# The last two outputs of three projections: whole products in the first half of the contraction, and another bank for the rest of the second token half

## The reference

```
for i in range(2):
    m = mixer_i(rmsnorm(x, norm_mix_pre[i]))           # ends in a projection to 1024
    x = x + rmsnorm(m, norm_mix_post[i])
    f = conv_ffn(rmsnorm(x, norm_ffn_pre[i]))          # ends in a projection to 1024
    x = x + rmsnorm(f, norm_ffn_post[i])
```

## Time and profile before

| | us |
|---|---|
| median of 3 runs | 1428.8 |
| range of the runs | 1427.78 to 1429.37 |
| profiled execution | 1427.95 |
| its span, first to last instruction | 1426.2 |
| PE busy | 1407.8 (99%) |
| DVE busy | 1003.5 (70%) |
| ACT busy | 623.4 (44%) |
| POOL busy | 112.3 (8%) |

### The profile page before, as it was taken

One profiled execution on the slowest core, in us unless ns is written; L12 is line 12 of the kernel. 1 busy time (PEld: TensorE's weight loads), 2 busy tenths in 40 slices (PEclk: granted clock), 3 DMA queues, 4 the chain that ended last, 5 costly groups with the idle time before them and its releaser, 6 DMA issues.

```text
span 1426.2 us, 21715 instructions
## 1 busy us (share of the span) xinstructions
PE 1407.8 (99%) x7526; PEld 1177.3 (83%) x7526; DVE 1003.5 (70%) x1510; ACT 623.4 (44%) x1019; POOL 112.3 (8%) x85
## 2 busy tenths in 40 slices
PE   8999999999999999999999999999999999999997
PEld 6888888888789888888888977777798888888887
DVE  6988888889437888888522676767488888886123
ACT  6666556557334323232323456556653232333221
POOL 0000000000110000000011032232110000000111
PEclk9999999999999999999999999999999999999999
DMA  4433433342231322323233012121212223233231
GB/s 165 180 135 128 147 117 118 136 142 76 83 139 33 102 98 94 103 88 114 102 100 141 31 60 75 59 74 59 93 56 89 97 94 103 89 108 103 102 101 60
DMA packets 37445, 142.34 MB, mean 100 GB/s; under 512 B 4176, under 2 KB 6352, under 8 KB 35344
## 3 DMA queue, kind: packets, MB, share of 16 engines
q1 hardware_dynamic: 37392, 141.63, 28.7%
HBM read 139.38 MB, written 2.23 MB: 99 GB/s over the span
## 4 chain that ended last, share of the span: by engine, by line
PE 94%; DVE 3%; ACT 1%; DMA 1%; issue 1%; SPq 0%; POOL 0%; POOLq 0%; ACTq 0%
PE bank L469 21%; PE bank L471 20%; PE bank L470 20%; PE b_x L469 7%; PE b_x L470 7%; PE b_x L471 7%; PE b_y L1073 1%; PE b_norm L1642 1%; PE b_y L469 1%; PE b_y L471 1%; DVE hn_lo L814 1%; PE b_y L470 1%; PE b_x L1085 1%; PE b_y L1076 1%; DVE mbuf L819 1%; PE b_cb L1602 1%
## 5 line engine op out<-in xcount | busy, mean ns | idle before, releaser
L417 ACT ACTIVATE w_hi<-raw 128x1024 fp32r<-128x1024 f32 (+1 forms) x201 | 222.8, 1108 | 403.2 <-PE bank L471 287.8
L432 DVE TENSOR_TENSOR w_lo<-raw,w_hi 128x1024 fp32r<-128x1024 f32 (+1 forms) x181 | 234.1, 1294 | 229.5 <-ACT w_hi L417 229.4
L469 PE MATMUL bank<-hn_hi,w_hi 128*128 128x512 f32 x848 | 337.2, 398 | 2.2 <-DVE w_lo L432 1.1
L471 PE MATMUL bank<-hn_hi,w_lo 128*128 128x512 f32 x848 | 330.8, 390 | 0.0
L470 PE MATMUL bank<-hn_lo,w_hi 128*128 128x512 f32 x848 | 330.3, 390 | 0.0
L469 PEld LDWEIGHTS bank<-hn_hi,w_hi 128*128 128x128 f32 x848 | 159.2, 188 | 40.0 <-issue 4.5
L471 PEld LDWEIGHTS bank<-hn_hi,w_lo 128*128 128x128 f32 x848 | 159.2, 188 | 33.9
L470 PEld LDWEIGHTS bank<-hn_lo,w_hi 128*128 128x128 f32 x848 | 159.4, 188 | 31.4
L469 PE MATMUL bank<-h_hi,w_hi 128*128 128x512 f32 (+1 forms) x352 | 127.9, 363 | 0.0
L471 PE MATMUL bank<-h_hi,w_lo 128*128 128x512 f32 (+1 forms) x352 | 127.6, 363 | 0.0
L470 PE MATMUL bank<-h_lo,w_hi 128*128 128x512 f32 (+1 forms) x352 | 127.6, 363 | 0.0
(11 more groups left out here) (318 smaller groups left out, 2423.1 us busy)
## 6 DMA issues: line engine op xcount, KB each, us to landing
raw<-w_up SPq DMA_DIRECT2D x80, 512.0 KB, 3.2
raw<-w_mix SPq DMA_DIRECT2D x48, 512.0 KB, 3.3
raw<-w_dn SPq DMA_DIRECT2D x32, 704.0 KB, 4.1
raw<-w_qkv SPq DMA_DIRECT2D x20, 512.0 KB, 3.3
acs_bc<-scratch SPq DMA_DIRECT2D x8, 1024.0 KB, 5.6
ecs_bc<-scratch SPq DMA_DIRECT2D x8, 1024.0 KB, 4.7
raw<-w_sout SPq DMA_DIRECT2D x16, 512.0 KB, 3.2
first_raw<-w_up SPq DMA_DIRECT2D x8, 512.0 KB, 6.3
```

The lines of the kernel that those rows point to most:

```text
L417: nc.scalar.activation(halves_of(ph, j if own else rep, own or first and j < 4)[0], raw_of(ph, rep, first and j < 4), ACT.Copy).then_inc(h ...
L432: nc.vector.tensor_tensor(lo, raw_of(ph, rep, first), hi.bitcast(F32), ALU.subtract).then_inc(lo_made, 1)
L469: nc.tensor.matmul(acc[:], wh, hi, start=first, stop=False)
L471: return nc.tensor.matmul(acc[:], wl, hi, start=False, stop=last)
```

## The change

Three projections (SOUT, DN0, DN1) are concerned. AOUT keeps its accumulators; in its boundary only the order in `wide_start` changes.

- `pair_pe`: the first half of the contraction of outputs 6 and 7 is made by products over all 512 tokens into the output's bank. The rest of token half 0 is added there. The rest of token half 1 begins anew in `b_x`.
- So token half 1 is the sum of two accumulators. ScalarE copies the bank's part to mbuf behind the root of token half 0 (semaphore `kept`). VectorE adds the part in `b_x` to it (`join`), and that is now what counts as the evacuation of the output. ScalarE's square of token half 1 waits for this and reads mbuf.
- `join` 0 stands on VectorE behind the first two new_x of token half 0, `join` 1 behind new_x of chunk 3. At the end of the kernel they stand ahead of the third group of scalings and ahead of the second reciprocal.
- `wide_start`: as `b_x` is read until the joins are done, chunks 0 and 1 are run for units 0 and 1 first, then the statistic of token half 1, then a wait for the evacuations, then chunks 0 and 1 for units 2 and 3.

```diff
         def part_acc(ph, t, s):
-            return acc_of(ph, s)[:, tokens(1)] if t else b_x[:, s, tokens(0)]
+            own = t if ph is AOUT else not t
+            return acc_of(ph, s)[:, tokens(t)] if own else b_x[:, s, tokens(t)]
@@ pair_pe
                     for c in range(tiles):
-                        for t in range(2):
-                            last = product(part_acc(ph, t, s), slot_of(ph, u), c, hi[:, c, tokens(t)],
-                                           lo[:, c, tokens(t)], c == 0, False)
+                        last = product(acc_of(ph, s), slot_of(ph, u), c, hi[:, c, :], lo[:, c, :], c == 0, False)
...
-                                       k == 0, c == tiles - 1)
+                                       c == 0 and (t == 1 or ph is AOUT), c == tiles - 1)
@@ wide_start
-            for c in range(KC):
+            for c in range(2):
+                for j in range(2):
+                    chunk(0, j, c)
+            part_stat(pe, b, 1)
+            pe.wait_ge(evac["out"], nxt.before["out"])
+            for c in range(2):
+                for j in (2, 3):
+                    chunk(0, j, c)
+            for c in range(2, KC):
                 for j in range(4):
                     chunk(0, j, c)
-                if c == 0:
-                    part_stat(pe, b, 1)
@@ boundary_act, take
+                if t and ph is not AOUT:
+                    act.wait_ge(evac["out"], ph.before["out"] + KC - 1 + s)
+                    nc.scalar.activation(sq[:, s, tokens(t)], mbuf[:, 2 * END + s, tokens(t)],
+                                         ACT.Square).then_inc(part_squared, 1)
+                    return
@@ boundary_act, behind part_root(0)
+            if ph is not AOUT:
+                for s in range(2):
+                    nc.scalar.activation(mbuf[:, 2 * END + s, tokens(1)], acc_of(ph, s)[:, tokens(1)],
+                                         ACT.Copy).then_inc(kept, 1)
@@ new, VectorE
+        def join(dve, b, s):
+
+            ph = PH[2 * b - 1]
+            if ph is AOUT:
+                return
+            dve.wait_ge(unit_done, ph.U0 + ph.units - 1 + s)
+            dve.wait_ge(kept, 2 * KEEPS.index(b) + s + 1)
+            nc.vector.tensor_tensor(mbuf[:, 2 * END + s, tokens(1)], mbuf[:, 2 * END + s, tokens(1)],
+                                    b_x[:, s, tokens(1)], ALU.add).then_inc(evac["out"], 1)
@@ boundary_dve
                 new_x(t, 0)
                 new_x(t, 1)
+                if t == 0:
+                    join(dve, b, 0)
                 for m in range(KC):
...
                     if m + 2 < KC:
                         new_x(t, m + 2)
+                    if t == 0 and m == 1:
+                        join(dve, b, 1)
@@ end_dve
                 if t:
+                    join(dve, b, 1)
                     part_diag(dve, b, t)
...
+                    if t == 0 and n == 2:
+                        join(dve, b, 0)
                     for m in steps:
                         scale(m)
```

More of the change, by code:

```diff
@@ L260, in trunk @@
         rpre_copied = sem("rpre_copied")
+        kept = sem("kept")
         scaled, x_new = sem("scaled"), sem("x_new")
@@ L567, in trunk @@
         END = KC // 2 - 1
+        KEEPS = (1, 2, 4)
         PARTS_POOL = (0, 2, 4, 5, 6)
@@ L874, in add @@
                                             ALU.add).then_inc(part_added, 1)
-                for steps in (((0, 1), (2, 3), (4, 5), (6, 7)) if t == 0 else ((0, 2, 1), (4, 3), (5, 6, 7))):
+                for n, steps in enumerate(((0, 1), (2, 3), (4, 5), (6, 7)) if t == 0 else
+                                          ((0, 2, 1), (4, 3), (5, 6, 7))):
+                    if t == 0 and n == 2:
+                        join(dve, b, 0)
                     for m in steps:
```

## The result

| | before | after |
|---|---|---|
| median of 20 runs each, us | 1428.62 | 1430.76 |
| lowest and highest | 1427.38, 1430.79 | 1429.27, 1432.73 |
| span of the profiled execution | 1426.2 | 1430.1 |

The ratio of after to before is 1.0014, with a 95% interval of 1.0008 to 1.0020: slower, by less than the 0.2% inside which I called a change none. The forecast was 1430.0.

The account below looks back on a forecast made before the run. TensorE, with 94% of the chain of waits, was taken to bound the kernel. The terms -1.76 + 2.0 + 0.1 + 0.0 + 0.9 = +1.2 us, added to the median 1428.8, gave 1430.0, range 1429.0 to 1431.3.

Parts of the forecast that it names:

- Mergers: First halves by whole products: 180 mergers save 0.0133 us each, 0.64 at SOUT, 0.88 each at DN0 and DN1.
- rival C: TensorE's first halves: merging gains nothing, a whole product taking 0.24 us; time 1431.8, chance 0.03.
- SOUT's gain lost on w_lo: SOUT's last unit: TensorE arrives 0.64 us earlier and waits 0.64 for the weights' w_lo, so SOUT gives 0.
- The same absolute time, 428.9: Sign at SOUT's last unit: TensorE's wait of about 0.6 us on w_lo ends at 428.9, as before.
- Boundary 1, 2.0: After SOUT: squares wait for joins queued on VectorE, its turn to the second token half moves; cost 2.0 us.
- Rival A: Inside boundaries: the queues hide the joins; time 1427.9, or 1427.3 if SOUT's 0.64 came through; chance 0.13.
- Boundary 2, 0.1: After DN0: last square ends 0.2 to 0.6 us before TensorE needs it; cost 0.1, between 0 and 0.6.
- rival B: Boundary 2: join 1 is late there as well, costing 1.4 us, and boundary 1 costs 3.2; time 1432.5, chance 0.11.
- Boundary 3, 0: AOUT's boundary: only TensorE's first chunk order changes, and hn_lo 1 still comes in time; cost 0.
- The end, 0.9: Kernel's end after DN1: joins delay the last square and nothing hides it; cost 0.9 us, between 0.5 and 1.7.
- Rival D: Boundary 1: the clock falls in the stall, 40 half products at 0.213 us add 3.7; about 1433.7, chance 0.03.

Follow-up runs that it names:

- SOUT alone: The change made at SOUT only, DN0 and DN1 as in the kernel before: median 1431.60 us, ratio to before 1.0013.
- the repetition: The changed kernel run once more with no edit, for a second profiled execution: median 1430.17 us, ratio to the kernel before 1.0012.
- DN1 alone: The change made at DN1 only, SOUT and DN0 as in the kernel before: median 1429.48 us, ratio to before 1.0002.
- all moves: Changed kernel, all three projections, with earlier chunk casts, earlier join 1 (also at the end) and SOUT's last weight cast earlier: 1426.76 us, 0.9982 to before.

## Why the prediction was right, and where not

- **Mergers.** Whole products at 0.2267, 10.88 us at SOUT; at DN0 and DN1 the way from the pair's first product to S0 is 25.20 before and 24.32 after, 0.88 each. Right; rival C is out.
- **SOUT's gain lost on w_lo.** The wait is there, 0.3 to 1.2 us where I had 0.6, and with the weights moved it is gone and the unit starts 0.70 earlier: shown. Counted from the start of the pair, TensorE took the unit up at 14.39 before, and at 14.24 to 14.35 in the five of seven profiles in which the weights landed as before. So 0.04 to 0.15 of the 0.64 came through, where I had 0. In the other two it is 14.72 and 15.07: the landing was late, which the forecast left out. "The same absolute time, 428.9" was wrong as a sign (428.2 to 429.9), since the start of the kernel moves all of it.
- **Boundary 1, 2.0.** Measured 1.98 without a fall of the clock, with the statistic 1.88 late where I had 1.85. Rival A is out. The path was as described, step by step. In the profile of after, 1.41 more come from the clock.
- **Boundary 2, 0.1.** Measured 0.00, with 0.25 of margin left; rival B is out.
- **Boundary 3, 0.** The list of TensorE's waits around it is empty in both kernels, and the turn stands at 15.34 from S0 in both.
- **The end, 0.9.** Measured 1.44. The mis-sized term: I moved join 1 and forgot what else join 0 moves. GpSimd's pass behind the square of output 6 now falls into a pair of additions, 0.76 becomes 1.24, and those 0.48 are the difference (0.9 + 0.48 = 1.4). I had counted this effect at boundary 1 and left it at the end to the upper bound, 1.7. The measured 1.44 is inside the bounds.
- **Rival D** had 0.03, too little. A fall of the clock stood in the first profile and in that of SOUT alone, and not in the repetition. Its price was over-estimated: 15 half products at 0.213, as that estimate had it for one, but not 40. The stalls that brought it down were shorter than the 0.6 to 1.2 us each that I had put: 0.34, 0.21 and 0.70.

The terms measured without a fall give -0.88 - 0.88 + 1.98 + 0 + 1.44 = +1.66, less the 0.04 to 0.15 that SOUT keeps: about +1.5 to 1.6, where the forecast's sum was +1.2. The medians moved by 2.14 in the first set and 1.25 in the repetition. So the forecast's largest error, the end too cheap by 0.5, is real and lies inside the scatter of the medians. The clock and the late landing were left out of the sum, and each is in some executions only. The first profile had both, which is why its span grew by 3.9: 0.4 from the start of the kernel, 0.7 at SOUT's last unit, 1.98 + 1.41 at boundary 1, 1.4 at the end, less 0.88 twice, and 0.2 less on the way from boundary 2 to the end that I did not follow.

What stays open is how often the clock falls in executions without a profile, and why the same three waits brought it down in two profiles and not in a third. For the changed kernel the mean clock of a run can't tell: with DN1 alone most runs show 0.997, as most of after do, from the longer idle end. SOUT alone has the end of before, and there it tells something: 4 of its 11 runs show 0.998, and 26 of the 35 of before. So a fall, at boundary 1 or at the start, is in some of its executions and not in others. The rows themselves are no full record either: in five profiles four to eight of the first whole products stand at 0.427 us while the windows read 1.00.

## What to carry to other kernels

Where an accumulation is split to save instructions on the bounding engine, look first at what must now be joined, and where that joining stands in its engine's written order: here 2.4 us of saved matmuls met 3.4 us of waits, and the same change with its joins, its first casts and one weight cast put earlier is 1.9 us faster than before. A saving only counts if the next thing wanted, here a cast of weights, is moved forward with it. And where an operation is delayed, follow also the engines that it starts: a GpSimd pass set going later stretched VectorE work on the path, where before it had been the one stretched. And before a time is put down to a change, look at where the execution stood ahead of the changed code: here the first 22 us alone scatter by up to 3.8.

## What the runs showed of the hardware

- TensorE's granted clock fell to 0.50, its lower level of 1.2 GHz, behind three waits of 0.34, 0.21 and 0.70 us within 3.2 us of each other, and 15 half products were issued at that level. Behind two such short waits and one of 4.06 us the rows show it down from the window 445:446 to 452:453. Among the kernel's first products it fell in two profiles, with SOUT alone (TensorE had stood 1.62 us before its product at 9.19) and with all moves (1.26 before the one at 9.02 and 0.38 before the one at 10.34); at the earlier trace rows, with waits of 0.96 and 1.07 us and 0.93 of 2 us busy, it had not. It stayed down for 3.3 us at boundary 1 in the first profile, and for 3.4 and 6.8 us among the first products. The Trainium skill (TensorE: Matmul & The Clock Gate, section A second HAM failure mode: psum-queue depth-cycling) describes a kernel in which frequent short idles between groups of matmuls bring the clock down. Two of the three profiles with these waits agree, by the 0.50 of their windows; the third, at 1.00, does not.
- VectorE operations that read two SBUF operands were held up by a GpSimd pass that started ahead of them: hn_lo 0.48 became 0.67 and 0.96, a pair of additions 0.76 became 1.24; with the pass at one column it was 0.76 again. Where the additions had started first, by 0.01 us (before, 1413.06), they took 0.75 and the pass took 1.35 in place of 0.73.
- The landing of one set of weights differed by 0.9 us between executions of nearly the same program. Counted from the start of SOUT's pair, ScalarE's cast behind it started at 10.74 to 10.84 in eight profiles with the same order of casts, and at 11.22, 11.56 and 11.66 in three. In those three TensorE took up the last unit 0.4 to 0.8 us late.
